# A hybrid attention and expert layer on one core: the input projection spread over the stages, and expert rows added with half-width weights

## The reference

```python
xn = rms_norm(x, attn_norm_g)
qa, ka, va, qb, kb, vb = jnp.split(xn @ w_in, ...)         # 1024 -> 3072
qa, ka, qb, kb = (apply_partial_rope(rms_norm(z, g), cos, sin) ...)
oa = rms_norm(dilated_mixture(qa, ka, va), out_norm_a)      # 8 heads
ob = rms_norm(diff_attention(qb, kb, vb, lam), out_norm_b) * (1 - lam_init)
h = x + concat([oa, ob]) @ w_out
hn = rms_norm(h, ffn_norm_g)
s = einsum(hn @ w_peer_q, sub_keys)                         # 8 heads, 2 x 128 keys
idx, gates = top 16 of the sums of the two top 16, softmax
act = gelu(einsum('cd,chkd->chk', hn, u_table[idx])) * gates
out = h + einsum('chk,chkd->cd', act, v_table[idx])
```

## Time and profile before

| | us |
|---|---|
| median of 3 runs | 3675.07 (3672.83 to 3680.99) |
| profiled execution | 3687.51 |
| its span | 3685.7 |
| until the first product of the projection | 19.2 |
| projection of eight tiles | 19.2 to 414 |
| front of tile 0, until the first dot product | 414 to 572 |
| stages 1 to 8, by each one's first dot product | 572, 919.5, 1300.8, 1683.8, 2068.2, 2459.2, 2854.3, 3267.1 |
| last dot product, end | 3634.2, 3685.7 |

### The profile page before, as it was taken

How to read it: one execution, slowest core, us unless ns; L and a number is a source line. 1 busy time by engine, 2 the same in 40 slices (tenths; PEclk the granted TensorE clock), 3 DMA queues, 4 the chain that set the end, 5 groups by cost and what they waited for, 6 DMA issues and landing times.

```text
span 3685.7 us, 29514 instructions
## 1 busy us (share of the span) xinstructions
PE 3044.6 (83%) x9440; PEld 1473.1 (40%) x9440; DVE 2061.8 (56%) x4508; ACT 762.7 (21%) x1695; POOL 2249.5 (61%) x2052
## 2 busy tenths in 40 slices
PE   7999665887988799878987898879887998766677
PEld 3444343442444244434443344435442544322223
DVE  1333257577556755675657565765577455754442
ACT  2111102211321132113211232123211321111111
POOL 0000006777777777777777777775777567777775
PEclk9999776999999999999999999999999999999999
DMA  5000237999999999999999999998999899999998
GB/s 175 23 23 17 106 103 282 384 406 370 373 378 406 373 359 378 406 384 356 356 404 406 345 345 385 406 365 311 377 405 376 279 327 403 381 356 368 365 365 307
DMA packets 351792, 1191.68 MB, mean 323 GB/s; under 512 B 41376, under 2 KB 41504, under 8 KB 351648
## 3 DMA queue, kind: packets, MB, share of 16 engines
q0 software_dynamic: 294912, 1073.87, 76.9%
q1 hardware_dynamic: 56736, 116.03, 8.6%
HBM read 1177.17 MB, written 12.58 MB: 323 GB/s over the span
## 4 chain that ended last, share of the span: by engine, by line
PE 42%; POOL 24%; DMA 20%; issue 9%; DVE 2%; another core or an unknown queue 2%; SPq 1%; ACT 1%; ACTq 0%; DVEq 0%
PE psum L590 21%; DMA big<-in_peer_v,big 18%; POOL big L408 12%; POOL big L417 11%; PE psum L446 8%; PE psum L501 3%; PE psum L566 3%; PE psum L530 2%; PE psum L545 2%; PE psum L517 1%; DMA big<-in_peer_u,big 1%; SPq L325 1%; DMA big<-in_x 0%; DMA big<-in_c_iota 0%
## 5 line engine op out<-in xcount | busy, mean ns | idle before, releaser
L590 PE MATMUL psum<-big 128*128 128x512 f32 x4096 | 2004.6, 618 | 478.6 <-DMA big<-in_peer_v,big 397.2
L1026 DVE CUSTOM_DVE_ANT_0 big<-big 128x1024 f32<-128x1024 f32 x1024 | 1247.3, 1225 | 854.7 <-DMA big<-in_peer_u,big 748.9
L408 POOL DMA_INDIRECT big<-in_peer_u,big x1024 | 1111.8, 1086 | 883.4 <-DVE big L953 567.1
L417 POOL DMA_INDIRECT big<-in_peer_v,big x1024 | 1137.4, 1111 | 540.9 <-PE psum L590 248.3
L590 PEld LDWEIGHTS psum<-big 128*128 128x128 f32 x4096 | 720.4, 192 | 1535.6 <-DMA big<-in_peer_v,big 803.5
L680 ACT ACTIVATE big<-ident,big 128x128 f32<-128x128 f32 x1024 | 394.9, 398 | 1878.9 <-PE psum L590 1357.9
L446 PE MATMUL psum<-big 128*128 128x512 f32 x768 | 339.4, 602 | 2.3 <-DMA big<-in_w_in 1.2
L566 PEld LDWEIGHTS psum<-big 128*128 128x128 f32 x2048 | 250.8, 195 | 61.7 <-issue 54.7
L839 DVE CUSTOM_DVE_ANT_0 big<-psum,big 128x128 f32<-128x128 f32 (+7 forms) x128 | 96.9, 757 | 308.7 <-PE psum L501 192.4
L566 PE MATMUL psum<-big 128*128 128x128 f32 x2048 | 253.2, 278 | 8.9 <-ACT big L729 5.6
L501 PE MATMUL psum<-KT,big 64*128 64x512 f32 (+3 forms) x384 | 170.2, 553 | 64.6 <-DVE big L839 46.0
(11 more groups left out here) (120 smaller groups left out, 1266.8 us busy)
## 6 DMA issues: line engine op xcount, KB each, us to landing
big<-in_w_peer_q SPq DMA_DIRECT2D x128, 512.0 KB
big<-in_peer_u,big POOLq DMA_INDIRECT x1024
big<-in_peer_v,big POOLq DMA_INDIRECT x1024
big<-in_w_in SPq DMA_DIRECT2D x6, 2048.0 KB, 17.8
big<-in_x SPq DMA_DIRECT2D x16, 512.0 KB, 3.7
q_scratch<-big SPq DMA_DIRECT2D x8, 512.0 KB, 2.8
big<-q_scratch SPq DMA_DIRECT2D x8, 512.0 KB
big<-in_w_out SPq DMA_DIRECT2D x1, 4096.0 KB, 15.1
```

The source lines that it names most:

```text
L408: nc.gpsimd.indirect_dma_start(out=u_ring[:, g % RU, :], out_offset=None, in_=peer_u, in_offset=bass.IndirectOffsetOnAxis(ap=idx[:, t % 2, ...
L417: nc.gpsimd.indirect_dma_start(out=v_ring[:, g % RV, :], out_offset=None, in_=peer_v, in_offset=bass.IndirectOffsetOnAxis(ap=idx[:, t % 2, ...
L590: last = nc.tensor.matmul(pAcc[:, n, :], diag[:, g % RD, :], v_ring[:, g % RV, n * COLS:(n + 1) * COLS], start=(p == 0), stop=(p == PICKS ...
L1026: v.tensor_tensor_reduce(out=row_, in0=row_, in1=hn[:, t % 2, :], scale=1.0, scalar=0.0, op0=ALU.mult, op1=ALU.add, accum_out=dot[:, t % 2 ...
```

## The change

The projection is cut into 96 *units*, each one tile times 256 columns of `w_in`. A table gives each unit its chunk, its load, its PSUM bank and its slot. Tile 0's 12 units stand in slots 3 to 14 of a new stage -1 of 18 slots, those of tiles 1 and 2 (24) in slots 16 to 56 of stage 0, those of tiles 3 to 7 (60) in the even slots 0 to 58 of stages 1 and 2. `w_in` is no longer kept: a chunk of 256 columns (1 MB, in pieces of 1 KB) is loaded once for tile 0, once for tiles 1 and 2 into a ring of five in the place of the row rings, and once for tiles 3 to 7 in four quarters into a single place. That place, the normed tiles 3 to 7 and the tables lie where `w_out` lay, so `w_out` is loaded in chunks of 128 rows through the query weights' ring for tiles 0 to 2, and whole at slot 1 of stage 3.

A q or k unit is squared and summed by ACT, one pass of 64 columns per head, scaled by ACT in four more passes, rotated by DVE, turned by PE three slots after its product and kept by ACT.

v rows are gathered by pairs of picks: gather c of a pair brings to partitions 0 to 63 and 64 to 127 the rows of two picks of the 64 tokens of half c. The weight is 128x64 (`sel`, from `folded`, two identities on top of one another), and a product writes the 64 partitions of its half. A pair is four products of 128x512, alternately for the two halves, and needs both of its ring slots. `weigh` writes `act` in four pieces and `expert_index` makes a second index table for it. `RD` goes from 4 to 6. Some constants move to ACT's DMA queue, and the additions of epsilon go into ACT's square root.

```diff
+CUT = 256
+PRE_SLOTS = 18
+EARLY_ORDER = Q_CHUNKS + K_CHUNKS + V_CHUNKS
+LOAD_CHUNKS = EARLY_ORDER + EARLY_ORDER + LATE_ORDER
+TILE_GROUPS = ((0,), (1, 2), (3, 4, 5, 6, 7))
...
+SLOTS_12 = tuple(range(0, 60, 2))
+X_PLACES = ((-1, 0), (-1, 15), (-1, 16), (0, 57), (0, 58), (0, 59), (0, 60), (0, 61))
...
+            def load_w_late(l, kq):
+                chunk = LOAD_CHUNKS[l]
+                if l > LATE_LOAD and kq < 3:
+                    sp.wait_ge(late_used, 3 * (l - 1 - LATE_LOAD) + kq + 1)
+                elif l > LATE_LOAD:
+                    sp.wait_ge(proj_ready, LAST_OF_LOAD[l - 1].n + 1)
...
+            def project(u):
+                if u.before is not None:
+                    pe.wait_ge(proj_kept, u.before + 1)
...
+                for k in range(KC):
+                    last = nc.tensor.matmul(bank[:, 0:CUT], xnT(u.tile)[:, k, :], w,
+                                            start=(k == 0), stop=(k == KC - 1), skip_group_check=True)
...
-                for n in range(2):
-                    last = nc.tensor.matmul(pAcc[:, n, :], diag[:, g % RD, :],
-                                            v_ring[:, g % RV, n * COLS:(n + 1) * COLS],
-                                            start=(p == 0), stop=(p == PICKS - 1))
-                last.then_inc(v_used.sem, 1)
+                for n in range(2):
+                    for c in range(PAIR):
+                        last = nc.tensor.matmul(pAcc[half_rows(c), n, :], sel[:, (g + c) % RD, :],
+                                                v_ring[:, (g + c) % RV, n * COLS:(n + 1) * COLS],
+                                                start=(p == 0), stop=(p == PICKS - PAIR), skip_group_check=True)
+                        if n == 1:
+                            last.then_inc(v_used.sem, 1)
...
+            def square_unit(u):
+                e.wait_ge(proj_ready, u.n + 1)
+                for h in range(4):
+                    last = e.activation(squares[:, h * HD:(h + 1) * HD], unit_bank(u)[:, h * HD:(h + 1) * HD], ACT.Square,
+                                        scale=SCALE, accum_out=mean_u[:, u.turn % 2, h:h + 1])
...
+                e.activation(rms_u[:, u.turn % 2], mean_u[:, u.turn % 2], ACT.Sqrt, bias=eps).then_inc(unit_root, 1)
```

More of the change, by code:

```diff
@@ new lines, in list_units @@
+def list_units():
+    places = [(-1, s) for s in range(3, 15)] + [(0, s) for s in SLOTS_0] + [(e, s) for e in (1, 2) for s in SLOTS_12]
+    units = []
+    for load, chunk in enumerate(LOAD_CHUNKS):
+        for tile in TILE_GROUPS[load // len(EARLY_ORDER)]:
+            units.append(Unit(len(units), tile, chunk, load, places[len(units)]))
+    turned = stored = 0
+    for u in units:
+        u.before = max((o.n for o in units[:u.n] if o.bank == u.bank), default=None)
+        u.turn = u.store = None
+        if not u.is_v:
+            u.turn, turned = turned, turned + 1
+        if u.is_q and u.tile:
+            u.store, stored = stored, stored + 1
+        u.first = all(o.load != u.load for o in units[:u.n])
+        u.last = all(o.load != u.load for o in units[u.n + 1:])
+    return units
@@ new lines, with unit_at, turns_of, stores_of @@
+UNITS = list_units()
+UNIT_AT = {u.slot: u for u in UNITS}
+LOADS = len(LOAD_CHUNKS)
+LATE_LOAD = min(u.load for u in UNITS if u.tile >= EARLY)
+LATE_UNIT = min(u.n for u in UNITS if u.tile >= EARLY)
+LAST_OF_LOAD = {u.load: u for u in UNITS if u.last}
+TURNS = sum(not u.is_v for u in UNITS)
+def unit_at(e, s, back):
+    return UNIT_AT.get(lin(e, s) - back)
+def turns_of(tile):
+    return 1 + max(u.turn for u in UNITS if u.tile == tile and not u.is_v)
+def stores_of(tile):
+    return 1 + max(u.store for u in UNITS if u.tile == tile and u.is_q)
@@ L45, with products_of, w_chunks, w_first @@
+def products_of(tile):
+    return 1 + max(u.n for u in UNITS if u.tile == tile)
+W_OUT_CHUNKS = KC
+def w_chunks(t):
+    return 2 * PH + (W_OUT_CHUNKS if t < EARLY else 0)
+def w_first(t):
+    return sum(w_chunks(i) for i in range(t))
+def w_place(t, i):
+    if t < EARLY:
+        if i < W_OUT_CHUNKS:
+            return lin(t, 21 + i // 2)
+        i -= W_OUT_CHUNKS
+    return lin(t, 27 + 6 * (i // 4) + i % 4)
+W_LIST = [(t, i) for t in range(TILES) for i in range(w_chunks(t))]
 class Signal:
@@ L393, in _ @@
                         load_qt(tf + 1)
[L394 to L397 removed]
+                    if tf is not None and s == 25:
+                        sp.wait_ge(h_ready.sem, h_ready.at(tf, 1))
+                        sp.dma_start(rows(h_dram, tf), hn[:, tf % 2, :]).then_inc(h_stored.sem, 16)
@@ L414, in gather_v @@
                 t, p = divmod(g, PICKS)
+                q, c = divmod(p, PAIR)
                 if g >= RV:
@@ L486, in scores, with bank_free @@
+            def bank_free(e, s, *banks):
+                done = [u.n for u in UNITS if u.bank in banks and u.slot < lin(e, s)]
+                if done:
+                    pe.wait_ge(proj_kept, max(done) + 1)
+                turns = [u.turn for u in UNITS if not u.is_v and u.slot + 3 < lin(e, s)]
+                if ("O", 1) in banks and turns:
+                    pe.wait_ge(turn_kept, max(turns) + 1)
             def scores(t, m):
                 if m == 0:
-                    pe.wait_ge(qt_loaded.sem, qt_loaded.at(t, 1))
@@ new lines, in keep_unit @@
+            def keep_unit(u):
+                bank = unit_bank(u)
+                if u.is_v:
+                    e.wait_ge(proj_ready, u.n + 1)
+                    last = e.activation(V[:, u.tile, u.part * CUT:(u.part + 1) * CUT], bank[:, 0:CUT], ACT.Copy)
+                else:
+                    e.wait_ge(unit_rms, u.turn + 1)
+                    if u.turn >= 2:
+                        e.wait_ge(unit_turned, u.turn - 1)
+                    for h in range(4):
+                        last = e.activation(raw[:, u.turn % 2, h * HD:(h + 1) * HD], bank[:, h * HD:(h + 1) * HD],
+                                            ACT.Copy, scale=rms_u[:, u.turn % 2, h:h + 1])
+                last.then_inc(proj_kept, 1)
```

737 lines of the change are left out of this document (424 added, 313 removed).

## The result

The changed kernel took 3510.6 us (median of 4 runs, 3506.3 to 3523.9), the kernel before 3675.2 beside it: a ratio of 0.956, interval 0.954 to 0.958. The forecast was 3440, in a range of 3375 to 3590. So it is faster by 165 us, and 71 slower than forecast. The profiled execution has a span of 3505.6 against 3685.7; the sum of the prediction made this 3449, so 57 us of span have to be found.

The account below looks back on a forecast made before the run. It took the DMA engines to bound the middle stages, after a serial projection. Its terms, 3685.7 - 284 + 77 + 25 - 58 - 7 + 10, made 3449 us of span, hence 3440 measured; range 3375 to 3590.

Parts of the forecast that it names:

- The serial part: Everything before the first dot product of a row: at 288 us instead of 572, so -284 us.
- The first part: From the start through tile 0's twelve units and the norms of tiles 1 and 2: over at 84 us.
- the query part: Tile 0's front from its query products to its first gather: 102 us with units, plus 9 for norm chains.
- Rival 2: Stage 0's front doesn't hold its units, PE waits and stays at 1.2 GHz: +70 us, 3510, chance 0.12.
- Bytes: Stages 1, 2 and 3: 25 MB of added weight loads, hidden by nothing, cost +77 us (33, 33, 11).
- Coupling: Stages 1 and 2: attention waits for ACT's table loads for q and k units, +15 and +10 us.
- The halves: Stages 4 to 7: both halves' products overlap fully, a pair takes 1.71 us, late slots shrink: -58 us.
- rival 1: Products of the two halves run one after the other, PE holds stages 1 and 2: 3555 us, chance 0.25.
- What pairs cost: v ring of five slots: a pair's slots come free together, less cover against jitter, +10 us in all.
- L may be 8: v ring: L is a gather's landing time; two pairs' 11.5 us would allow 8, against 11 before.
- Rival 4: Five v slots in pairs starve the gathers if landings stay at 11 us: +730, about 4170, chance 0.06.
- The tail: The last 24 v rows, 51.5 us before, become 7 us shorter.

Follow-up runs that it names:

- e4: The changed kernel without eleven of the twelve late loads of w_in and the waits for them (output wrong): ratio 0.9485 to the kernel before.
- e5: The changed kernel with the reciprocal of a unit's norm moved behind both dot products of its slot on DVE: ratio 0.9525 to the kernel before.
- e0: The changed kernel itself, unchanged, run again as the base of the second group: ratio 0.9581 to the kernel before.
- e6: The changed kernel with six v and four u ring slots and the norm's reciprocal behind the dot products: ratio 0.9428 to the kernel before.
- e3: The changed kernel with six v and four u ring slots instead of five and five: ratio 0.9596 to the kernel before.
- e7: The changed kernel with full-width v rows, one pick at a time, and the norm's reciprocal behind the dot products: ratio 0.9588 to the kernel before.
- e1: The changed kernel with v rows added as before, full width and one pick at a time: ratio 0.9624 to the kernel before.
- e2: The kernel before with only pairs and halves added, its projection as it was: ratio 1.0087 to the kernel before.
- e10: The kernel of e6, unchanged, run again in the third group: ratio 0.9498 to the kernel before.

## Why the prediction came out as it did

Point by point, in the order of its sum; misses in us of span add up to the 57.

**The serial part: +12.5.** The first part ended at 84, to the microsecond, partly by luck: the first product came at 29.0 and not 26 (the queue of before has a second issue of 3.52 us, which I had overlooked), and the twelve units and what follows them took 3 less than I had. The rest was short by little: attention and `w_out` took 83.0 where I had 25 + 48 + 5, the query part 116.7 where I had 102 + 9, and from the first gather to the first dot product 16.8 for 15. The units cost about what I had worked out. Of attention's part, one unit stands between the last products of attention (107.1 to 111.7 us), for which I had added nothing, and attention is 29 us for 25; the 6 us of the query part aren't placed. Rival 2 is refuted: the granted clock there is 0.81 and 0.91, above the 0.75 of before, and the part is 216.5 long.

**Bytes: right, +3, in part by luck.** Shares times lengths of the queue that carries the weights, before and after: 25.0 and 65.1 us in stage 1, 29.0 and 62.6 in stage 2, 29.1 and 35.7 in stage 3, so +40, +34 and +7, 80 in all for a forecast of 77. The unknown price of a 1-KB piece was 51 to 52 ns, some 315 GB/s (e4), 6.8 MB costing 21 to 22 us instead of the 17.9 at 381 GB/s: nearer to the full rate, as taken. But that queue moved 27.8 MB more in these three stages, not 25; the stores of q by units, 20 of 128 KB in stage 1, are among what I had left out. This is its row of stage 1 before, to set beside the one after at e4:

```profile
q1 hardware_dynamic: 4640, 9.44, 7.2%
```

**Coupling: +4, and +3 in stage 3.** What is left of stages 1, 2 and 3 beyond the bytes is 12, 17 and 3 us, for 15, 10 and 0. The size was right, the mechanism was not, and that is luck: ACT's table loads are there, but they are 1.28 of the 9.98 us shown at e5. Most of the wait is a chain, PE's unit, then ACT, then DVE's reciprocal, which I had counted as work and not as a place to stand. Moving the reciprocal (e5 against e0) takes 20 us out of stages 1 and 2, of the 29 that are to be explained here; with four u slots (e6 against e3, of two groups) it is 55.

**The halves: mechanism right, size wrong, +37.** This is the term that failed: -58 became -21 in stages 4 to 7. That a pair takes the time of one pick is shown (1.94 us for eight records), and rival 1 is refuted. PE's part came too, by a rough measure: in stage 7, busy time times granted clock fell from 353.2 x 0.98 = 346 to 286.3 x 0.84 = 240, 106 for the 64 x 1.71 = 109 expected. The Trainium skill, TensorEngine Tiling (Array Packing), Key Properties, says that tiles work independently, and that holds here. Its other rule, that a change of tiling mode drains the engine, I had worked out at 35 us a stage if each change cost a pick's tail. Attention's slots in stage 7 give a bound. From 2720 to 2754 us PE has no idle time in them, and a slot goes from turn to turn in 6.73 us:

```profile
2726.90 1.09 PE L684 MATMUL psum<-ident,big 128*128 128x128 f32 x8
...
2733.63 1.09 PE L684 MATMUL psum<-ident,big 128*128 128x128 f32 x8
```

Before it was 8.20; less a pick's 1.71 that is 6.49, and less its 1.98 with the tail 6.22. So I estimate two changes of mode at 0.24 us together and at most 0.51, 15 to 33 us of PE in 64 slots, which is under the 35.

What the halves should give, they gave where PE was late: over the first 124 us of stage 7, which hold attention, the DMA share is 0.94 at 336 GB/s, where it was 0.83 at 285 in the 131 us of before.

```profile
2691.00:2815.00 124.00, 111.63 (x510) 55.00 (x506) 77.09 (x143) 48.91 (x89) 83.38 (x77) 0.93 0.94 336
```

But I had taken off the whole excess over 381, although my own 6.5 us a slot was still above the 5.96 of the DMA engines. With 6.73 in 16 slots of attention that alone is an estimated 12 us in stage 7, and less in the stages before it.

A second cause is the ring: five slots in pairs take back 12 to 21 us of stages 4 to 7 in the first group, 16 and 18 in the second and 8 in the third, each within its group (six slots come with four u slots in all of them). The third is the one whose gathers are as slow as in the forecast's run, so 8 is the nearest to what the ring cost there. The rest isn't isolated. With six slots these stages sum to 1524 in the first group, which is the 381 apiece that I had forecast, and to 1534 and 1571 in the others. So the floor of 381 can be reached with this front, and what holds the stages near 390 where gathers are slow stays open.

**What pairs cost: the working was wrong.** I had +10 in all. It was 8 to 21 in stages 4 to 7, and in the last stage, which I had left at nothing because its share was 0.97 already, 12 and 24 in the second group (343.5 and 355.8 with five slots, 331.6 with e7's full width), 19 in the first, and 2.5 in the third, there against six slots. In the forecast's own run my reading of that row did hold, 365.2 for 367, which was luck: the gathers happened to be slow. The step that failed is "it has to fit into 2 pairs, 11.5 us, then, so L may be 8". It used the pace of that slow stage and PE's time at the full clock; at e1's pace two pairs are 10.4 us, and with PE's 3.0 us at the lower clock only 6.1 are left for a landing, just about the 6.2 that e2 shows. e2 is a loss of 0.9%: where the rest of the kernel is as before, pairs with five slots cost more than the halves give. Rival 4 had this mechanism, but at 730 us.

**The tail: +9.** It was to lose 7 and gained 2. POOL's gathers in order of time, after:

```profile
3456.06 0.94 POOL L570 DMA_INDIRECT big<-in_peer_v,big  x1 [3.24 <-PE psum L774]
...
3494.99 0.94 POOL L570 DMA_INDIRECT big<-in_peer_v,big  x1 [3.15 <-PE psum L774]
```

POOL waits up to 3.4 us for PE to free a pair, and from the first row to the last it issues a gather every (3494.99 - 3456.06)/20 = 1.95 us. Before, PE freed one slot every 1.72 us. A PE that adds rows twice as fast made this loop slower, as its slots come back in twos. With six slots the tail is 46.3, 46.5 and 44.7 (e3, e6, e10) against 51.5 to 54.7 with five, and full width has 47.5 with five (e1).

The rest is the last stage at -2, and the 10 for pairs that the sum held apart: 12.5 + 3 + 4 + 3 + 37 - 2 + 9 - 10 = 57. The predicted side and range were right because the one large term, 284, was right to 4%; e1 and e7 show that nearly all of the gain is the projection's.

## What to carry to other kernels

When two operations are fused so that they return buffers together, count the ring anew, with the pace of the fastest stage and the engine's time at the clock that it will be granted. Here a ring of five that gives back two at a time kept some 4.5 gathers in flight where one that gives back one at a time kept 7, and where PE wasn't late that cost more than halving PE's work gained.

A step that waits for another engine belongs behind the work in its queue that frees buffers, even if the step itself takes 0.2 us.

When a faster engine is to take away an excess, compare its new time per slot with the next limit, slot by slot. And read a floor from more than one group of runs: the same stages were 381 us apiece in one and 393 in another.

## What was unexpected of the hardware

With less to do, PE was granted less in the last stage: the mean granted clock was 0.98 with PE busy 257.6 of 367.1 us and 0.69 with 199.1 of 365.2, so part of the pairs ran at 1.2 GHz, 3.31 us instead of 1.94. The busy share alone doesn't tell the clock, though: e2's tail has 1.00 with PE busy 25.2 of 51.5 us. No run isolates what the lower clock costs; e6 reached the shortest last stage of all at 0.70.

The same kernel's gathers ran at 409 GB/s in the last stage of one group and at 368 in another (e6 and e10, 329.0 and 366.0 us), both on chip 15, and the kernel before moved along, 3611 and 3692 us. No run tells why. A ratio measured in one of them held for the other only to 0.7%.
